# The attention loop of a hybrid encoder step: half projections as a stream, later sample turns, weights' low parts on GpSimd, turns at the head of each step

## What is computed

```python
def fox_attention(q, k, v, cq, ck, q_pos, k_pos):
    ...
    def one_block(args):
        qblk, cblk, pblk = args
        s = jnp.einsum('bqhd,bkhd->bhqk', qblk, k).astype(jnp.float32) * scale
        s = s + (cblk[:, :, :, None] - ck_t[:, :, None, :])
        causal = pblk[:, None] >= k_pos[None, :]
        s = jnp.where(causal[None, None], s, -jnp.inf)
        p = jax.nn.softmax(s, axis=-1)
        return jnp.einsum('bhqk,bkhd->bqhd', p.astype(v.dtype), v)
```

## Time and profile before

| | us |
|---|---|
| median of 3 runs | 934.71 |
| lowest and highest | 930.95, 934.89 |
| the profiled execution | 929.26 |
| its span in the profile | 927.5 |
| the attention loop, from the first scores to the last values | 67.8 to 225.4 |
| TensorE busy, of the span | 865.8 (93%) |
| VectorE, ScalarE, GpSimd busy | 545.6, 371.6, 90.5 |

### The profile page before, as it was taken

How to read it: one execution, slowest core, us unless ns; L and a number is a source line. 1 busy time by engine, 2 the same in 40 slices (tenths; PEclk the granted TensorE clock), 3 DMA queues, 4 the chain that set the end, 5 groups by cost and what they waited for, 6 DMA issues and landing times.

```text
span 927.5 us, 16044 instructions
## 1 busy us (share of the span) xinstructions
PE 865.8 (93%) x6119; PEld 830.1 (90%) x6119; DVE 545.6 (59%) x979; ACT 371.6 (40%) x588; POOL 90.5 (10%) x156
## 2 busy tenths in 40 slices
PE   5988778888799999999999999999999999999996
PEld 4887767778799789998998999999999999999996
DVE  2887776685766457556567665523555542355644
ACT  6574565453733545434334333311233321133324
POOL 5025251441100002000000000000000000000000
PEclk9999999999999999999999999999999999999998
DMA  6355432313532754210232332232332232322122
GB/s 200 110 174 136 115 95 67 82 46 112 171 90 81 289 174 137 69 47 23 69 90 70 91 90 80 79 90 70 90 90 69 79 90 80 91 69 89 51 85 104
DMA packets 116506, 91.21 MB, mean 98 GB/s; under 512 B 3136, under 2 KB 107798, under 8 KB 116211
## 3 DMA queue, kind: packets, MB, share of 16 engines
q1 hardware_dynamic: 111331, 73.51, 26.4%
q0 software_dynamic: 5136, 17.17, 6.1%
HBM read 81.32 MB, written 9.35 MB: 98 GB/s over the span
## 4 chain that ended last, share of the span: by engine, by line
PE 75%; DVE 11%; ACT 5%; issue 4%; DMA 3%; SPq 0%; ACTq 0%; DVEq 0%
PE ps L393 61%; PE ps L2045 3%; PE ps L2101 2%; PE ps L1795 1%; PE ps L2051 1%; PE ps L2130 1%; ACT w_hi L414 1%; PE ps L2151 1%; DMA wp_raw<-in_w_pool 1%; DVE prob_p L1442 1%; DMA x_tok<-in_x_sample 1%; DMA w_raw<-in_w_mk 1%; DVE pt L423 1%; DVE y_tok L1756 1%; PE ps L1918 1%
## 5 line engine op out<-in xcount | busy, mean ns | idle before, releaser
L419 DVE TENSOR_TENSOR w_lo<-w_raw,w_hi 128x1024 fp32r<-128x1024 f32 x109 | 133.8, 1228 | 174.1 <-ACT w_hi L414 172.0
L393 PE MATMUL ps<-a_hi,w_hi 128*128 128x288 f32 x1024 | 222.6, 299 | 8.9 <-DVE q_lo L426 5.1
L393 PE MATMUL ps<-a_lo,w_hi 128*128 128x288 f32 x1024 | 220.3, 297 | 0.0
L393 PE MATMUL ps<-a_hi,w_lo 128*128 128x288 f32 x1024 | 220.2, 297 | 0.0
L414 ACT ACTIVATE w_hi<-w_raw 128x1024 fp32r<-128x1024 f32 x109 | 114.9, 1054 | 189.0 <-PE ps L393 179.3
L393 PEld LDWEIGHTS ps<-a_hi,w_hi 128*128 128x128 f32 x1024 | 166.9, 190 | 13.2 <-issue 9.3
L393 PEld LDWEIGHTS ps<-a_lo,w_hi 128*128 128x128 f32 x1024 | 166.2, 190 | 0.0
L393 PEld LDWEIGHTS ps<-a_hi,w_lo 128*128 128x128 f32 x1024 | 166.1, 190 | 0.0
L393 PE MATMUL ps<-b_hi,w_hi 128*128 128x288 f32 x576 | 123.9, 297 | 1.7 <-DVE b_lo L426 1.7
L393 PE MATMUL ps<-b_hi,w_lo 128*128 128x288 f32 x576 | 123.4, 296 | 0.0
L393 PE MATMUL ps<-b_lo,w_hi 128*128 128x288 f32 x576 | 123.3, 296 | 0.0
(11 more groups left out here) (361 smaller groups left out, 1268.2 us busy)
## 6 DMA issues: line engine op xcount, KB each, us to landing
w_raw<-in_w_up SPq DMA_DIRECT2D x44, 512.0 KB, 3.7
w_raw<-in_w_down SPq DMA_DIRECT2D x16, 512.0 KB, 3.7
w_raw<-in_w_in SPq DMA_DIRECT2D x15, 512.0 KB, 4.1
w_raw<-in_w_o SPq DMA_DIRECT2D x8, 512.0 KB, 3.7
w_raw<-in_w_mq SPq DMA_DIRECT2D x8, 512.0 KB, 3.7
w_raw<-in_w_mo SPq DMA_DIRECT2D x8, 512.0 KB, 3.8
w_raw<-in_w_mk SPq DMA_DIRECT2D x6, 512.0 KB, 3.2
w_raw<-in_w_down SPq DMA_DIRECT2D x8, 384.0 KB, 3.3
```

Source lines behind the costliest of these rows:

```text
L393: mm = nc.tensor.matmul(acc[:, h, 0:H], w[slot][:, c], x[:, k, h * H:h * H + H], start=(k == first and w is w_hi and x is x_hi), stop=(k = ...
L419: nc.vector.tensor_tensor(w_lo[slot][:], w_raw[slot][:], w_hi[slot][:].bitcast(F32), ALU.subtract).then_inc(weight_lo_ready, 1)
```

## The change

- `FILL` gives way to `UNITS`: a unit is the three matmuls of one feature tile for one half (288 tokens). The table says how many units a step has (4, 4, 3, 3, ... in pair 0; from step 10 on 3, 4, 4, 1, 1, 4, 3, 3, 3, 3, 3 per pair). One half's eight tiles run first, then the other's. `finish_half` reads a half out in the step after it is complete; `half_done` and `half_free` pass it on.
- `turn_step`: the sample's three entries are turned at s + 4 instead of s + 3; the values follow one step later, as for all.
- On TensorE the order in a step becomes scores, turns, units, values. On ScalarE the turned high parts now stand before the exponentials.
- The low parts of the weight blocks 8 to 13 move from VectorE to GpSimd (`weights_low`). Blocks 14 and 15 stay.
- The mask's row lands inside `decay_p`, at block 7, and serves as the fourth tile's own run; three blocks are then copied and the four diagonal blocks masked in two operations. The load waits until the scores have used the old table. On VectorE, which expands head 0 of pair 0, the largest copy goes.
- GpSimd's order changes with it, and some buffers change their place.

The diff, cut to its core:

```diff
+    def turn_step(g):
+        return g + LAG + (g % ENTRIES >= 2 * NT)
...
-    FILL = {0: (0, [0, 1]), 1: (0, [2, 3]), 2: (0, [4]), 3: (0, [5]), 4: (0, [6, 7]),
-            6: (1, [0, 1, 2]), 7: (1, [3]), 8: (1, [4, 5]), 9: (1, [6, 7])}
+    UNITS = [4, 4, 3, 3, 3, 3, 3, 3, 3, 3]
+    for j in range(1, PAIRS):
+        UNITS += [3, 4, 4, 1, 1, 4, 3, 3, 3, 3, 3]
...
+    def halves_after(s):
+        return [u // KT for u in fill_units(s - 1) if u % KT == KT - 1] if s >= 1 else []
...
+            def weights_low(n):
+                pool.wait_ge(weight_hi_ready, n + 1)
+                pool.wait_ge(weight_lo_ready, n)
+                nc.gpsimd.tensor_tensor(w_lo[n % 2][:], w_raw[n % 2][:], f32(w_hi[n % 2][:]),
+                                        ALU.subtract).then_inc(weight_lo_ready, 1)
...
             for s in range(STEPS):
                 j, e = divmod(s, ENTRIES)
-                if e in (5, 10) and j < PAIRS:
-                    if j + 1 < PAIRS:
-                        (finish_q, finish_k)[e // 10](j + 1)
+                for i in halves_after(s):
+                    finish_half(i)
...
-                if s < N_ENTRIES and e < ENTRIES - 1:
-                    exponentials(s)
                 for t in turns_of(s):
...
-                if s < N_ENTRIES and e == ENTRIES - 1:
-
+                if s < N_ENTRIES:
                     exponentials(s)
...
-                if weights_after(s) is not None:
-                    rest_of_weights(dve, weights_after(s), weights_after(s) % 2)
+                n = weights_after(s)
+                if n is not None and n >= W_U + 2:
+                    dve.wait_ge(weight_lo_ready, n)
+                    rest_of_weights(dve, n, n % 2)
...
+                for u in fill_units(s):
+                    n, half, _, _ = half_task(u // KT)
+                    k = u % KT
+                    if k == 0:
+                        if half == 0:
+                            pe.wait_ge(weight_lo_ready, n + 1)
+                        if n == W_QK + 2:
+                            pe.wait_ge(acc_free, A_QK + 2)
+                        elif half == 0:
+                            pe.wait_ge(half_free, n - W_QK - 2)
+                        else:
+                            pe.wait_ge(acc_free, A_QK + n - W_QK)
+                    for w, x in ((w_hi, a_hi), (w_hi, a_lo), (w_lo, a_hi)):
+                        ins = mm(ACC[0][:, half, 0:H], w[n % 2][:, k * P:k * P + P], x[:, k, half * H:half * H + H],
+                                 start=(k == 0 and w is w_hi and x is a_hi), stop=(k == KT - 1 and w is w_lo))
+                    if k == KT - 1:
+                        ins.then_inc(weight_used if half else half_done, 1)
```

168 lines of the change are left out of this document (107 added, 61 removed).

## The result

| | before | after |
|---|---|---|
| median | 932.85 us (11 runs) | 924.17 us (11 runs) |
| lowest and highest | 930.95, 938.84 | 920.94, 929.91 |
| the profiled execution | 929.26 | 925.55 |
| the attention loop in it | 157.66 | 151.73 |
| TensorE busy | 865.8 | 866.7 (94% of 923.8) |

The ratio is 0.9904, with a 95% interval of 0.9884 to 0.9924: 8.7 us less by the medians. The forecast was 22.1 us less, a time of 912.6 and a range of 902 to 924; the time lies just above it. The direction is right, the size is not: 8.7 is under half of 22.1. The forecast was taken from 934.71, the median of three executions; over eleven the kernel before has 932.85, so on that base it would have been 910.8.

The account below looks back on a forecast made before the run. The attention loop was taken as bound by handovers, no engine full. Savings of 3.4 (pair 0), twice 5.1, 5.7 (pair 3) and 2.8 (drain), together 22.1 us, taken from 934.71 gave 912.6 us, range 902 to 924.

Parts of the forecast that it names:

- Projections as a stream: In the attention loop, one half is read out while the other runs: the 1.87 us wait on q's read-out goes.
- Sample a step later: Before the first sample turn: scale ends 5.0 to 6.2 us after the score, 1.0 of the 2.26 us wait left.
- Step 3: In a steady pair, the second turn waits for the low part of the turn two back: about 1.8 us.
- Turns at the head: In a steady pair, units nearly cover a turned tile's parts: waits of 1.05, 0.85 us and three small ones go.
- Step 6: In a steady pair, TensorE waits 0.45 us for the second cached-key turn's low part.
- Step 9: In a steady pair, the values wait 0.6 us behind the half of k and another held scale.
- Low weights on GpSimd: Per pair, VectorE gains 2.5 us from two low weights moved and gives 3.0 to holds by GpSimd, 1.5 each.
- The VectorE rival: All four long GpSimd operations of a pair hold VectorE, 2.5 us a pair more than counted: 923 us, chance 0.16.
- Work without waits: TensorE's work in a steady pair, counted start to start where no gap is: 27.3 us.
- Clock: Low clock charged: 1.5 us in pair 0, 0.9 in pair 3, 1.0 in the drain, none in pairs 1 and 2.
- Pair 3: Last head pair, 37.4 us before: work 26.1, waits 4.2, half clock 0.9, window sums 0.5, so 31.7, 5.7 less.
- Behind the loop: Pool weights' load, mixing and their 2.07 us wait shift with the last values: no gain, no loss.

Follow-up runs that it names:

- The kernel with least waits: Changed kernel with ScalarE's output copy ahead of its exponentials, GpSimd's long operations in pieces and ScalarE's weight rounding a step later: 905.6 us, ratio 0.9699.
- the even units: Units spread evenly (3 in every step, 2 in the last) on the changed kernel with output copy first and GpSimd in pieces: 908.5 us, ratio 0.9723.

## Why the prediction was wrong, by its steps

The loop was forecast at 28.3 + 31.3 + 31.3 + 31.7 + 13.1 = 135.7 us and measured 151.7 in the profiled execution, 16 more. Of these, TensorE's idle time in pairs 1 to 3 is 20.5 (5.6, 6.2, 8.7) against waits of 12.2, which makes 8.3; its busy time there is 88.4 against 82.1 (work, clock and window sums), which makes 6.3; pair 0 has 0.9 and the drain 0.5. The step that failed is thus first of all the term of TensorE's waits, 4.0 a pair against 5.6, 6.2 and 8.7: the sample, step 9 and step 9 of pair 3. The second is the work of a pair, too small by 1.5 us even at full clock, and the third is that no low clock was charged in pair 1 (1.4).

- **Projections as a stream: right.** The wait of 1.87 on q is gone and no half's bank is waited for. What I placed "beside TensorE's work" was the failure: the halves' copies and ScalarE's rounding ahead of them sit on VectorE's path at steps 3 and 9.
- **Sample a step later: right in kind, mis-sized.** 1.0 was taken, 1.76 to 2.30 measured. The text had named both causes, VectorE's lag and the output copy behind the exponential; the chain ended 7.0 us after the score, outside the 5.0 to 6.2 worked out. Moving that one copy gave 7.2 us.
- **Step 3: the size was right, 1.8 against 1.67** in pair 2, in part by luck. The rounding, the half of q and the low parts are as counted, but the held scale isn't: it took 0.52, and without the low weight the wait is still 1.51. What made up for it is q's low part, 0.93 where 0.7 was counted, and a start 0.2 later. What was not drawn from it is the clock behind it.
- **Turns at the head: right where it had been read,** since the 0.85 ahead of the next pair became 0.17; the 1.05 on the cached keys was only replaced by step 3's. Undoing it cost 3.1 us and not 6 to 8.
- **Step 6: 0.45 against 0.68, and 0.45 more** a step later behind the held scale of 2.06. **Step 9: 0.6 against 1.49.** The count took a hold as a mean of 1.5 us per low weight; the one that mattered was the values' low part, which the change had not added.
- **Low weights on GpSimd:** counted as 2.5 less and 3.0 more for VectorE, that is near nothing; putting them back cost 2.9 us. Cutting all of GpSimd's long operations into pieces gave 2.7, 5.7 or 10.1 us, by what else was in order. The VectorE rival named the right engine and, at 923, came near the time, but its price was to be 2.5 us a pair from holds alone; the runs show an order on ScalarE as large.
- **Work without waits: 27.3 was 1.0 to 1.5 us short.** The kernel with least waits has 30.42 - 2.16 = 28.3 a pair, the changed one 35.02 - 6.22 = 28.8 in pair 2. Sums of starts taken where there is no gap leave out what each gap adds: nine projection matmuls take 1.27 us in that pair where no wait follows, 1.42 to 1.45 where one does, and there are seven waits. The sum has a slip too: by its own rates the 38 value matmuls are 5.0 us and not 5.4, so that the rates alone give 26.9.
- **Clock: none was charged in pairs 1 and 2,** because the earlier trace rows shows 1.00 there. But those rows are of one execution, with 0.989 over the whole run, and others of the same kernel go down to 0.978; the kernel before with the low weights on GpSimd has 0.91 and 0.95 in these pairs, 0.91 where no wait is over 0.05 us longer. So low clock there need not come from the change, and the prediction's base, a median 5.4 us above the execution that it read, may hold some of it; no trace of a slower execution of the kernel before is there to show it.
- **Pair 3:** TensorE waits 2.50 for a turned tile while VectorE works beside GpSimd's window sums (0.5 was charged), and this wait stays between 2.3 and 3.0 in every edit of the changed kernel but the even units (1.40). It is the largest term that the sum didn't see, and no edit was aimed at it.
- **The drain (13.1 against 13.6) and pair 0 (28.3 against 29.2,** with 1.25 on the cached keys' first load, not in the sum) held.
- **Behind the loop:** no change was forecast, and growth named as a sign of being wrong. These stages grew by 1.5 us in the profiled executions; why is open.
- **Masks:** nothing was charged, and no wait of TensorE names them; no run prices them.

The structure of the sum was fit for its purpose: with two orders on ScalarE put right and GpSimd's operations cut, a steady pair comes to 30.4 us and the whole to 905.6. What failed was to take small estimated waits as the end of it, each on a chain of several engines whose slack had been counted to a few tenths of a microsecond.

## What to carry to other kernels

When a change takes a queue's order apart and puts it together again, write for each in-order engine what is ahead of the one instruction that TensorE will wait for, and move out whatever is not due: here a copy of 0.59 us, a rounding of 1.04 us and three long GpSimd operations carried 18.5 us between them. Fix them together before judging any of them: the pieces were worth 2.7, 5.7 or 10.1 us and the late rounding 1.3, 3.4 or 8.7, by what stood beside them. And price a wait on TensorE by what may follow it, not by its length alone.
